# One step of a hybrid decoder trunk: the experts' up products one expert ahead of their down products, with a ring of weight buffers

## What is computed

```python
h  = rms_norm(x, g_mix) * (1 + sc_a) + sh_a
x  = x + gt_a * (concat(retention(h), mlstm(h)) @ w_out)
h2 = rms_norm(x, g_ffn) * (1 + sc_f) + sh_f
# top 4 of 32 experts for each token, softmax over the four logits
hu   = xe @ w_up[e] + b_up[e]                 # w_up[e]: 1024 x 2048
gate = minimum(hu[:, :1024], 7);  lin = clip(hu[:, 1024:], -7, 7)
ye   = ((lin + 1) * gate * sigmoid(1.702 * gate)) @ w_down[e] + b_down[e]   # 1024 x 1024
x    = x + gt_f * sum over the token's experts of gate weight * ye
```

## Time and profile before

| | before |
|---|---|
| median of 3 runs | 1354.84 us |
| profiled execution | 1354.65 us |
| its span, first to last instruction | 1352.8 us |
| mean granted TensorE clock | 0.954 of full speed |
| TensorE busy, with waits inside matmuls | 1219.4 us (90%) |
| VectorE / ScalarE / POOL busy | 390.5 / 221.8 / 72.6 us |
| moved by DMA | 465.61 MB, mean 344 GB/s |
| chain that ended last | TensorE 61%, DMA 20%, SyncE's queue 10% |

### The profile page before, as it was taken

How to read it: one execution, slowest core, us unless ns; L and a number is a source line. 1 busy time by engine, 2 the same in 40 slices (tenths; PEclk the granted TensorE clock), 3 DMA queues, 4 the chain that set the end, 5 groups by cost and what they waited for, 6 DMA issues and landing times.

```text
span 1352.8 us, 23254 instructions
## 1 busy us (share of the span) xinstructions
PE 1219.4 (90%) x8796; PEld 563.0 (42%) x8797; DVE 390.5 (29%) x850; ACT 221.8 (16%) x369; POOL 72.6 (5%) x148
## 2 busy tenths in 40 slices
PE   5999999979699999998899998899877998997895
PEld 4655457634433344442244443344222343342342
DVE  0173214653722122321122222212212232221126
ACT  3012242001301111111110111111111111111111
POOL 1010011450000000000000000000000000000002
PEclk9999999888899999998899998899988998998998
DMA  9836234673368999999999999999999999999992
GB/s 368 341 130 253 99 120 187 172 243 137 126 250 344 422 422 414 423 422 422 422 422 422 373 423 422 422 421 391 422 422 422 422 422 422 422 421 422 422 422 109
DMA packets 79956, 465.61 MB, mean 344 GB/s; under 512 B 8594, under 2 KB 26326, under 8 KB 27826
## 3 DMA queue, kind: packets, MB, share of 16 engines
q1 hardware_dynamic: 76898, 458.86, 83.4%
q10 hardware_dynamic: 2640, 5.68, 1.3%
q0 software_dynamic: 384, 0.59, 0.1%
HBM read 458.35 MB, written 6.16 MB: 343 GB/s over the span
## 4 chain that ended last, share of the span: by engine, by line
PE 61%; DMA 20%; SPq 10%; DVE 3%; issue 3%; POOL 2%; ACT 1%; POOLq 0%; DVEq 0%; ACTq 0%
DMA mem<-in_w_up 19%; PE psum L968 16%; PE psum L1004 11%; SPq L405 10%; PE psum L1014 8%; PE psum L624 6%; PE psum L939 4%; PE psum L605 3%; PE psum L811 2%; PE psum L461 2%; PE psum L628 2%; PE psum L732 1%; DMA mem<-in_mod_chunks 1%; PE psum L749 1%; PE psum L1036 1%
## 5 line engine op out<-in xcount | busy, mean ns | idle before, releaser
L968 PE MATMUL psum<-mem 128*32 128x512 f32 (+2 forms) x2432 | 415.6, 641 | 77.9 <-DMA mem<-in_w_up 66.9
L968 PEld LDWEIGHTS psum<-mem 128*32 128x32 f32 (+2 forms) x2432 | 115.1, 124 | 370.1 <-issue 202.6
L1004 PE MATMUL psum<-mem 128*32 128x512 f32 (+3 forms) x1024 | 213.7, 594 | 0.0
L1974 DVE TENSOR_SCALAR mem<-psum 128x256 f32<-128x256 f32 (+3 forms) x32 | 19.2, 601 | 592.6 <-PE psum L972 592.6
L1014 PE MATMUL psum<-mem 128*128 128x512 f32 (+1 forms) x396 | 156.9, 607 | 3.6 <-issue 1.9
L1993 DVE TENSOR_TENSOR mem<-mem,psum 128x1024 f32<-128x1024 f32 (+1 forms) x96 | 100.3, 1045 | 100.1 <-PE psum L1014 100.1
L1004 PEld LDWEIGHTS psum<-mem 128*32 128x32 f32 (+3 forms) x1024 | 81.3, 127 | 105.2 <-issue 96.4
L939 PEld LDWEIGHTS psum<-mem 128*128 128x128 bf16 x2304 | 79.3, 99 | 18.9 <-issue 18.6
L1339 ACT ACTIVATE mem<-mem 128x256 f32<-128x256 f32 (+3 forms) x32 | 17.9, 559 | 422.3 <-DVE mem L1974 422.3
L624 PE MATMUL psum<-mem 128*128 128x512 f32 x192 | 84.2, 595 | 0.0
L939 PE MATMUL psum<-mem 128*128 128x64 bf16 (+1 forms) x2304 | 83.2, 197 | 0.0
(11 more groups left out here) (262 smaller groups left out, 839.5 us busy)
## 6 DMA issues: line engine op xcount, KB each, us to landing
mem<-in_w_up SPq DMA_DIRECT2D x256, 1024.0 KB, 25.2
mem<-in_w_down SPq DMA_DIRECT2D x128, 1024.0 KB, 18.3
mem<-in_mod_chunks SPq DMA_DIRECT2D x12, 2048.0 KB, 12.1
mem<-in_in_chunks SPq DMA_DIRECT2D x8, 2048.0 KB, 8.8
mem<-in_out_chunks SPq DMA_DIRECT2D x2, 2048.0 KB, 10.2
mem<-in_x_prompt ACTq DMA_DIRECT2D x2, 1024.0 KB, 7.4
mem<-in_state_ret SPq DMA_DIRECT2D x4, 512.0 KB, 6.7
mem<-in_state_mlstm_c SPq DMA_DIRECT2D x4, 512.0 KB, 9.0
```

Source lines behind the costliest of these rows:

```text
L968: last = pe.matmul(out, xg[:, c, cols], moving, start=(c == 0), stop=False)
L1004: last[c] = pe.matmul(psum[slots * q:slots * q + slots, 6 + u, :], turned, piece_slot(UP + c, 2, D)[:, piece % 2, 512 * u:512 * u + 512], ...
```

## The change

Loads and uses follow one order: up(0), up(1), down(0), up(2), down(1), ..., up(31), down(30), down(31). The twelve slots become a ring in that order: up pieces of expert 0 in slots 0 to 7, of all later ones in 8 to 11 and 0 to 3; down pieces in 4 to 7, those of the last expert in 8 to 11. TensorE's loop body for expert e does up(e), gather(e+1), scatters 0 and 1, down(e-1), turning of the activations of e (into banks 4 and 5), turning of the gate weights, scatter 2. The first expert (`first_expert`) and the last down products (`last_down`) stand outside the loop, and the wait for `added` and `G_ready` ahead of `up` is kept only for over 64 rows, and not for the first expert. POOL picks a second selector, `bsel_down`. VectorE's and ScalarE's loops are shifted likewise: gate weights and additions of expert e-1 stand behind the SwiGLU of e.

For up to 64 rows the up products take the columns of `w_up` by parity (every second word), so that the activations lie contiguous for the turning, and row block `j * tiles + q` of `w_down` is used instead of `q * pieces + j`: pieces are used in the order in which they are loaded. A column with zero is put behind the 32 counts.

In the finish the order of the token tiles is 2, 0, 1; for the two prompt tiles the gate is multiplied onto `yd` before the last scatter (`yd_gated`), which leaves one addition a tile; and SyncE issues one store a tile.

The diff, cut to its core (empty lines are left out too):

```diff
+        def up_slot(c, first):
+            return c if first else (UP + c) % PIECES
+        def down_slot(c, last):
+            return UP + c if last else DOWN + c
...
+            def load_up(e, c, first):
+                s = up_slot(c, first)
+                sp.dma_start(piece_slot(s, 2 * D), a["w_up"][0][e, 128 * c:128 * c + 128, :]).then_inc(piece_in[s], 16)
+            def load_down(e, c, last):
+                s = down_slot(c, last)
+                src = a["w_down"][0][e, 256 * c:256 * c + 256, :].rearrange("(p h) n -> p h n", h=2)
+                sp.dma_start(piece_slot(s, 2, D), src).then_inc(piece_in[s], 16)
+            def load_ahead(e, it):
+                for c in range(4):
+                    sp.wait_ge(piece_done[up_slot(c, False)], it - 1)
+                    load_up(e, c, False)
+            def load_rest(e, it):
+                for c in range(4, UP):
+                    sp.wait_ge(piece_done[up_slot(c, False)], it)
+                    load_up(e, c, False)
+                for c in range(DOWN):
+                    sp.wait_ge(piece_done[down_slot(c, False)], it)
+                    load_down(e - 1, c, False)
+            def load_end(uses):
+                for c in range(DOWN):
+                    sp.wait_ge(piece_done[down_slot(c, True)], uses)
+                    load_down(NE - 1, c, True)
...
-                expert_piece(0, 2 * c)
-                expert_piece(0, 2 * c + 1)
-            with sp.Fori(1, NE) as e:
-                for c in range(PIECES):
-                    sp.wait_ge(piece_done[c], e)
-                    expert_piece(e, c)
+                for s in (2 * c, 2 * c + 1):
+                    if s < UP:
+                        load_up(0, s, True)
+                    else:
+                        load_up(1, s - UP, False)
+            load_rest(1, 1)
+            with sp.Fori(2, NE) as e:
+                load_ahead(e, e)
+                load_rest(e, e)
+            load_end(NE - 1)
...
-                if slots in (32, 96):
+                if slots == 32:
+                    w = weights.rearrange("p (l j c i h) -> p l j c i h", l=2, j=2, c=2, h=2)
+                    return [(psum[32 * q:32 * q + 32, 0, :], slice(0, 32), w[:, :, :, q // 2, :, q % 2]) for q in range(4)]
+                if slots == 96:
                     w = weights.rearrange("p (l n) -> p l n", l=2)
                     return [(psum[32 * q:32 * q + 32, g, :], slice(32 * g, 32 * g + 32), w[:, :, 256 * q:256 * q + 256])
                             for g in range(slots // 32) for q in range(4)]
                 if slots == 64:
                     return [(psum[64 * q:64 * q + 64, lin, :], slice(0, 64),
-                             weights[:, D * lin + 512 * q:D * lin + 512 * q + 512])
+                             weights[:, D * lin + q:D * lin + D:2])
                             for lin in range(2) for q in range(2)]
...
+            def up(ig, it, slots, first):
+                pe.wait_ge(S("xg_ready"), ig + 1)
+                if slots > 64 and not isinstance(it, int):
+                    pe.wait_ge(S("G_ready"), it + 1 if first else it)
+                    pe.wait_ge(S("added"), 3 * it + 1 if first else 3 * it - 2)
                 for c in range(UP):
-                    pe.wait_ge(piece_in[c], 16 * (it + 1))
-                    for out, cols, moving in up_products(slots, piece_slot(c, 2 * D)):
+                    s = up_slot(c, first)
+                    pe.wait_ge(piece_in[s], 16 * (it + 1) if first or c >= 4 else 16 * it)
+                    for out, cols, moving in up_products(slots, piece_slot(s, 2 * D)):
                         last = pe.matmul(out, xg[:, c, cols], moving, start=(c == 0), stop=False)
-                    last.then_inc(piece_done[c], 1)
+                    last.then_inc(piece_done[s], 1)
                 pe.wait_ge(S("bsel_ready"), it + 1)
                 for out, cols, moving in up_products(slots, bparts[:, 0:2 * D]):
                     last = pe.matmul(out, bsel[:, cols], moving, start=False, stop=True)
                 last.then_inc(S("up_done"), 1)
...
-                            piece = q * pieces + j
+                            piece = j * tiles + q
...
+            def first_expert(ig, it, count, count_next):
+                by_size(pe, count, lambda slots: up(ig, it, slots, True))
+                gather(ig + 1, count_next, None if isinstance(it, int) else it)
+                if not isinstance(it, int):
+                    pe.wait_ge(S("y_copied"), it + 1)
+                by_size(pe, count, lambda slots: turn_activations(it, slots, True))
+            def expert(r, e, it, count, count_before, count_next):
                 ig = r * (NE + 1) + e
-                pe.wait_ge(S("xg_ready"), ig + 1)
-                pe.wait_ge(S("G_ready"), it + 1)
-                pe.wait_ge(S("added"), 3 * it + 1)
-                by_size(pe, count, lambda slots: up(it, slots))
-                gather(ig + 1, count_next)
-                pe.wait_ge(S("y_copied"), it + 1)
+                n = it - 1
+                by_size(pe, count, lambda slots: up(ig, it, slots, False))
+                gather(ig + 1, count_next, it)
+                pe.wait_ge(S("G_ready"), n + 1)
+                pe.wait_ge(S("y_copied"), n + 1)
+                pe.wait_ge(S("added"), 3 * n + 1)
                 pe.wait_ge(S("gate_ready"), it + 1)
                 pe.wait_ge(S("lin_clipped"), it + 1)
-                scatter(it, 0)
+                scatter(n, 0)
                 pe.wait_ge(S("xg_ready"), ig + 2)
-                scatter(it, 1)
-                by_size(pe, count, lambda slots: turn_activations(it, slots))
-                pe.wait_ge(S("Pg_ready"), it + 1)
-                pe.wait_ge(S("added"), 3 * it + 2)
-                for t in range(NT):
-                    n = ROWS[t]
-                    last = pe.transpose(psum[:, 2, tok(t)], Pg[0:n, t, :], ident[0:n, 0:n])
-                last.then_inc(S("Pg_turned"), 1)
-                scatter(it, 2)
-                by_size(pe, count, lambda slots: down(it, slots))
+                scatter(n, 1)
+                by_size(pe, count_before, lambda slots: down(n, slots, False))
+                pe.wait_ge(S("added"), 3 * n + 3)
+                by_size(pe, count, lambda slots: turn_activations(it, slots, False))
+                turn_weights(n)
+                scatter(n, 2)
+            def last_down(n, count):
+                pe.wait_ge(S("G_ready"), n + 1)
+                pe.wait_ge(S("y_copied"), n + 1)
+                pe.wait_ge(S("added"), 3 * n + 1)
+                scatter(n, 0)
+                pe.wait_ge(S("actT_ready"), n + 1)
+                scatter(n, 1)
+                turn_weights(n)
+                scatter(n, 2)
+                by_size(pe, count, lambda slots: down(n, slots, True))
             def last_scatter(its):
                 pe.wait_ge(S("G_ready"), its + 1)
-                pe.wait_ge(S("y_copied"), its + 1)
                 pe.wait_ge(S("added"), 3 * its + 1)
-                for t in range(NT):
-                    if t == 2:
-                        pe.wait_ge(S("added"), 3 * its + 2)
-                    scatter(its, t)
+                for u in range(2):
+                    pe.wait_ge(S("y_copied"), its + 1 + u)
+                    last = pe.matmul(psum[64 * u:64 * u + 64, 0, :], G[:, tok(2)], yd[:, u, :], start=True, stop=True)
+                last.then_inc(S("last_scattered"), 1)
+                pe.wait_ge(S("y_gated"), 2)
+                for t in range(2):
+                    for u in range(2):
+                        last = pe.matmul(psum[:, 2 + 2 * t + u, :], G[:, tok(t)], yd_gated[:, u, :], start=True, stop=True)
+                    last.then_inc(S("last_scattered"), 1)
...
+            def copy_last(n, end):
+                copy_weights(n)
+                for c in range(DOWN):
+                    act.wait_ge(piece_done[down_slot(c, True)], n + 1)
+                if not end:
+                    act.copy(yd.rearrange("p u n -> p (u n)"), flat(6, D)).then_inc(S("y_copied"), 1)
+                    return
+                act.copy(yd[:, 0, :], psum[:, 6, :]).then_inc(S("y_copied"), 1)
+                act.wait_ge(S("y_gated"), 1)
+                act.copy(yd[:, 1, :], psum[:, 7, :]).then_inc(S("y_copied"), 1)
...
+                for c in range(DOWN):
+                    dve.wait_ge(piece_done[down_slot(c, True)], its)
+                TT(yd_gated[:, 1, :], psum[:, 7, :], gateF_p[:, 512:D], ALU.mult).then_inc(S("y_gated"), 1)
+                dve.wait_ge(S("y_copied"), its + 1)
+                TT(yd_gated[:, 0, :], yd[:, 0, :], gateF_p[:, 0:512], ALU.mult).then_inc(S("y_gated"), 1)
+                dve.wait_ge(S("last_scattered"), 1)
+                for u in range(2):
+                    cols = slice(512 * u, 512 * u + 512)
+                    last = TT(acc[0:64, 2, cols], psum[64 * u:64 * u + 64, 0, :], gateF_s[0:64, cols], ALU.mult)
+                finish_step(last)
```

(15 more changed lines are left out.)

325 lines of the change are left out of this document (182 added, 143 removed).

## The result

The changed kernel takes 1360.41 us (median; 1356.73 to 1367.82), beside 1355.00 for the kernel before on the same chip: a ratio of 1.0051, 95% interval 1.0035 to 1.0067. It is slower by half a per cent. Forecast were 1337.2 us, 1.3% faster. The profiled execution spans 1358.1 us, 5.3 more than before and 22.8 more than the forecast span of 1335.3.

The account below looks back on a forecast made before the run. Weight transfers at about 421 GB/s bound the expert stage. Gains of 3.1, 2.9, 7.6, 3.2 and 3.0 make 19.8 us; less 2.3 for the tail, 17.5, giving 1337.2 us; range 1332 to 1342, chance 0.55.

Parts of the forecast that it names:

- (a): First up products: the first expert no longer waits for the memset of `acc`, starting at 366.2; gain 3.1 us.
- (b): First expert's up products: shorter TensorE idling avoids the fall to half clock; gain 2.9 us, bounds 0 and 2.9.
- (c): First experts' load order: a slot falls free earlier, so the queue gets its 21st piece 7.6 us sooner.
- (d): Next three slots: freed at 0.9 us each instead of 3.54, faster than pieces land; gain 3.2 us.
- R1: Rival: part comes; clock falls, later dips stay or TensorE limits experts 3 to 7; 1342 to 1347 us, chance 0.20.
- (e): Later queue dips: splitting the longest stretch without a freed slot gains 3.0 us, half of 6.1.
- (f): TensorE's tail: 24.1 us from last up piece to last down products; 2.3 of the 19.8 us given back.
- S: Start of the last down products: forecast at 1308.5 us, 17.5 sooner than the kernel before.
- (g): Finish, from the last down products to the end: still 26.8 us, no gain.
- (h): Up products of up to 64 rows: strided moving reads cost nothing, ratio 1.0, bounds 1.0 and 1.39.
- R3: Rival: strided moving reads slow up products, at ratio 1.39 giving 1372 us; decides from about 1.2; chance 0.09.
- (i): Third count, `bsel_down` and one more wait on `added` hide; uncovered, up to 1 us an expert on TensorE.

Follow-up runs that it names:

- layout run: Changed kernel with TensorE's branches laid out with the programs for many rows ahead of those for few: 1352.05 us, ratio 0.9993.
- ten lean experts: Changed kernel, TensorE's first ten experts written straight with only their own row count's code, loop from expert 10: 1344.25 us, ratio 0.9938.
- lean runs with parity: Changed kernel with only each expert's own row-count code on TensorE, for ten, nineteen or all experts: 1344.25, 1342.37, 1345.19 us.
- lean run with nineteen experts: Changed kernel, TensorE's first nineteen experts written straight with only their own row count's code, loop from expert 19: 1342.37 us, ratio 0.9919.

## Why the prediction was wrong, step by step

The sum of the miss, in the profiled execution: 22.8 us = 2.3 (start) + 21.2 (the down pieces' delay) - 0.3 (the rest of the stream and the tail) - 0.4 (finish). The -0.3 isn't measured but what is left over, if the whole delay of the down pieces reaches the end.

(a) **Start.** The memset's wait went as said, but 368.46 came instead of 366.2. What the products wait for, `xg`, was there 0.7 us sooner than forecast (363.93 + 1.01 = 364.94 for 365.63), and from there to the products it took 3.5 us where the step took 0.6 for the branch; in the layout run it is 0.05 (366.17 to 366.22). The 0.6 had no row behind it.

(b) **The clock.** For that reason TensorE idled 4.57 us again, and the up products took 22.14. With 1.10 us idle, in the layout run, they took 20.81 (forecast 20.8). The mechanism was right and depended on (a).

(c), (d) **The queue's order.** This is the step that failed. By the forecast's durations the 21st piece leaves 27.9 us behind the first up products (399.2 + 0.9 less what (a), (b) save, less 366.2) and the next down pieces 44.3: expert 1's up products from 27.0, then 7.1 for them, 0.3 bias, 2.1 gather, 3.5 scatters, 0.5 bias and 3.8 to the first freed slot. With ten lean experts it is 28.2 and 45.3; in the changed kernel 32.9 and 65.5. So the arithmetic of products and slots was good to 1 us, and what it left out is 21 us: the pauses (13.6), and products at the lower clock, which beside the run with ten lean experts take 1.3 us more in the first up products, 1.6 in the gather and 2.9 in the scatters. I had costed the new code of the first expert and of the loop's first pass at nothing, since no row before showed such a cost; the row that hinted at it, the 1.88 us of "issue" ahead of the scatters, I used for the clock only. "TensorE waits for something other than pieces between the experts" was named as what would make the prediction wrong, without a price or a rival. The Trainium skill's section on instruction fetch, quoted above, is a rule against this change that I did not weigh; with it, a rival of "some taken branches in the first pass, each uncovered" should have stood beside R1.

(e) **Later dips.** 3.0 of 6.1 us was right as a number: in the changed kernel they are 0.8 (407 GB/s, 475 to 500 us) and 2.2 (384, 525 to 550), 3.0 left. It is in part luck. The two large dips of before, at 765 to 780 and about 930 us, are gone altogether, and those left lie earlier, behind the hole; half was a choice, not a working.

(f) **Tail.** Forecast 24.1 us from the last up piece to S; measured 24.2. The copies cost 1.49 where 1.7 were taken.

(g) **Finish.** Forecast 26.8, measured 26.35: no gain worth the name, as said. Inside it errors cancel: 18.8 us to the last square for 18.1, 3.1 from there to the scaling for 3.6, and 3.2 for the store instead of 3.8.

(h) **Parity.** Taken at a ratio of 1.0; it is 1.03 for 64 rows and 1.06 for 32, worth 1 to 3 us, far from the 1.2 from which R3 decides. The rule of the Trainium skill, "SBUF — State Buffer", section "Door 1: The DMA port swizzle", that two hits on a 16-byte line run at full rate, isn't what these rows show for an fp32 moving operand at every second word: 616 ns against 595.

(i) **What hides.** No run tested it by itself; no row contradicts it.

Of the rivals, R3's sign came, by another mechanism. R1's limit, TensorE's run of experts 3 to 7, shows faintly at most: the lean runs with parity have 390 to 394 GB/s from 500 to 525 us, a loss of 1.6 to 1.8 us, and 419 to 423 from there to 650. The last 7.5 us between the lean run with nineteen experts (949.8) and the forecast (942.3) are: 3.3 of fade (the last up piece's products start at 1289.4, 24.1 ahead of S, and the bytes end (331 + 82) x 5/421 = 4.9 us behind 1300, so 15.5 for 18.8), an estimate of 1.3 for 34 more packets than before (0.56 MB at 421 GB/s), and 1.0 for the down pieces (45.3 for 44.3). The dips, with one of 1.0 at the loop's entry (417 GB/s, 900 to 1000 us), come to 3.2, for 3.0 in the forecast. Some 1.7 stay open, of which the parity may be 0.7.

## What to carry to other kernels

A change of order that adds a copy of code, or puts branches over code of other sizes right behind each other, has to be costed for the first pass through that code, not only for the instructions that run: look for what long work in the kernel before covers the fetches (here a lone "issue" bracket of 1.88 us was the only sign), and ask whether it still stands ahead of them. When a pause has no releaser, look whether an instruction packet lies in it. A loop's first pass belongs where the engine would wait anyway. A stall of 14 us costs more than 14 where a ring drains behind it and the clock falls.

## What the runs showed of the hardware

- TensorE's pauses at code that it enters or jumps over for the first time: 2.2 to 4.8 us each in the changed kernel, up to 8.08 with another layout, 5.11 at the entry of a loop; none in the same experts once the unused code was left out.
- An instruction packet of 16 KB, about 1 us long, lies in each pause of the changed kernel, and products start again 1.5 to 2.0 us behind its end. Thirty later passes of the same loop fetch none (439.5 to 1330 us).
- Pieces in the queue lengthen the three last pauses (11.4 us with the queue full, 11.9 with two pieces out at a time, 4.6 with it held), but alone make none (the kernel before with pieces loaded twice).
- An fp32 moving operand at a stride of two words: 616 ns a record of 64 rows for 595, 7.52 us for 7.07 in 64 records of 32 rows.
- More instruction packets (72 for 31) go with a stream that fades over 15 us at its end and a last up piece 4.7 us late for its place in it; with 44 packets there is no fade. What links the two isn't shown.
